# A three-block transformer kernel: at four stage changes the next stage takes up token rows 0 to 127 first

## Time and profile before

| | |
|---|---|
| median of 3 runs | 1083.47 us (1080.76 to 1084.18) |
| the profiled execution | 1084.3 us, its span 1082.3 us |
| TensorE busy | 1023.9 us, 95% of the span |
| VectorE, ScalarE, GpSimd busy | 611.3, 473.3, 352.5 us |
| HBM read | 174.6 MB |
| granted clock, mean over the span | 0.975 |

### The profile page before, as it was taken

The page is one execution under the profiler, slowest core; times in us unless marked ns, Lnnn a source line. Parts: engine busy times, 40 slices in busy tenths (PEclk is TensorE's granted clock), DMA queues, the critical chain, the costliest instruction groups (busy, mean ns, idle before and its releaser), DMA issues.

```text
span 1082.3 us, 16830 instructions
## 1 busy us (share of the span) xinstructions
PE 1023.9 (95%) x6908; PEld 897.5 (83%) x6908; DVE 611.3 (56%) x599; ACT 473.3 (44%) x606; POOL 352.5 (33%) x332
## 2 busy tenths in 40 slices
PE   7898789999999998999999999999978999999997
PEld 5886578999987877777779999987946979999986
DVE  3689855555564446354556755445467564554444
ACT  4465435444443355545454444434423554344432
POOL 3663054888899604030039910000031010000000
PEclk9999889999999999999999999999987999999999
DMA  9542014676666755443445656555971446556550
GB/s 353 170 156 78 1 43 140 217 220 216 225 210 215 244 177 160 148 159 117 138 154 159 191 158 190 194 194 192 378 267 41 143 130 191 161 191 194 178 172 39
DMA packets 130034, 186.85 MB, mean 173 GB/s; under 512 B 4672, under 2 KB 103488, under 8 KB 129344
## 3 DMA queue, kind: packets, MB, share of 16 engines
q1 hardware_dynamic: 105696, 158.34, 44.9%
q10 hardware_dynamic: 24288, 27.81, 7.7%
HBM read 174.60 MB, written 15.73 MB: 176 GB/s over the span
## 4 chain that ended last, share of the span: by engine, by line
PE 74%; DVE 11%; POOL 6%; ACT 4%; issue 3%; DMA 1%; POOLq 0%; SPq 0%; ACTq 0%; DVEq 0%
PE ps L362 11%; PE ps L364 11%; PE ps L363 11%; PE ps L405 7%; PE ps L409 7%; PE ps L407 7%; PE ps L379 3%; PE ps L381 3%; DVE cacc L1645 3%; PE ps L380 3%; DVE wlo L348 3%; PE ps L435 2%; POOL otmp L636 2%; ACT whi L342 2%; POOL ob L650 2%
## 5 line engine op out<-in xcount | busy, mean ns | idle before, releaser
L348 DVE TENSOR_TENSOR wlo<-wraw,whi 128x2048 fp32r<-128x2048 f32 x145 | 351.3, 2423 | 323.3 <-ACT whi L342 323.2
L342 ACT ACTIVATE whi<-wraw 128x2048 fp32r<-128x2048 f32 x145 | 277.5, 1914 | 294.2 <-PE ps L409 143.0
L362 PE MATMUL ps<-actH,whi 128*128 128x256 f32 x1248 | 357.8, 287 | 8.4 <-DVE wlo L348 6.3
L364 PE MATMUL ps<-actH,wlo 128*128 128x256 f32 x1248 | 354.9, 284 | 0.0
L363 PE MATMUL ps<-actL,whi 128*128 128x256 f32 x1248 | 354.8, 284 | 0.0
L362 PEld LDWEIGHTS ps<-actH,whi 128*128 128x128 f32 x1248 | 241.4, 193 | 12.4 <-DVE wlo L348 7.3
L363 PEld LDWEIGHTS ps<-actL,whi 128*128 128x128 f32 x1248 | 241.5, 194 | 0.0
L364 PEld LDWEIGHTS ps<-actH,wlo 128*128 128x128 f32 x1248 | 241.3, 193 | 0.0
L494 POOL TENSOR_SCALAR rs<-ss 128x1 f32<-128x1 f32 (+2 forms) x27 | 9.0, 334 | 611.7 <-ACT nat L477 487.0
L405 PE MATMUL ps<-whi,gH 128*128 128x512 f32 x264 | 82.3, 393 | 0.0
L409 PE MATMUL ps<-whi,gL 128*128 128x512 f32 x264 | 82.1, 392 | 0.0
(11 more groups left out here) (309 smaller groups left out, 1369.7 us busy)
## 6 DMA issues: line engine op xcount, KB each, us to landing
wraw<-in_ffn_w_gate SPq DMA_DIRECT2D x22, 1024.0 KB, 5.3
wraw<-in_ffn_w_up SPq DMA_DIRECT2D x22, 1024.0 KB, 5.3
wraw<-in_ffn_w_down SPq DMA_DIRECT2D x22, 1024.0 KB, 4.9
wraw<-in_fox_w_in SPq DMA_DIRECT2D x16, 1024.0 KB, 5.5
wraw<-in_w_gate SPq DMA_DIRECT2D x11, 1024.0 KB, 5.3
wraw<-in_w_up SPq DMA_DIRECT2D x11, 1024.0 KB, 5.6
wraw<-in_w_down SPq DMA_DIRECT2D x11, 1024.0 KB, 4.9
wraw<-in_w_in SPq DMA_DIRECT2D x10, 1024.0 KB, 7.3
```

The costliest lines, as they stand in the source:

```text
L342: act.activation(self.whi[:, n0 % RING, :], self.wraw[:, n0 % RAW, :], ACT.Copy).then_inc(self.hi_done, 1)
L348: dve.tensor_tensor(self.wlo[:, n0 % RING, :], self.wraw[:, n0 % RAW, :], self.whi[:, n0 % RING, :].bitcast(F32), ALU.subtract).then_inc(s ...
L362: pe.matmul(out, wh, self.actH[:, k, :], start=(i == 0), stop=False)
L364: last = pe.matmul(out, wl, self.actH[:, k, :], start=False, stop=(i == KT - 1))
```

## The change

- Buffers: four of `whi`, and `wlo` lies in the same four buffers as `wraw` (the low part is written over the raw unit). A load now waits until the unit four before is used up; a high part waits only for its landing.
- `mm_k_last`: the last two units of o1, f1, o2, f2, o3 and f3 are multiplied for row block 0 together, then for row block 1.
- At o1 to f1, o2 to f2 and o3 to f3 the first pair of the FFN is computed in token form (`pe_pair_rows`): row block 0 is turned in tiles of 128 tokens and multiplied with the gate and the up unit, then row block 1. The product is made from rows (`act_pair_rows`, `dve_pair_rows`) and turned by four transposes (`pe_turn_pair`) behind the next gate unit. At f1 to fox the two units fox and fox+1 are taken row block by row block in the same way.
- The diagonal is made by GpSimd (`pool_rows`). The order of norm, turn and splits in the streams of ScalarE and VectorE is new (`act_rows`, `rows`, `rows_post`).
- `keep_warm`: none before f1 and fox, 4 before f2 and f3, 17 before s as before.
- Table blocks: TensorE takes block b up after pair b+1 (blocks 0 to 9), and blocks 10 to 15 after down units 0, 2, 4, 6, 7, 8. `pool_prep` is not changed.
- fox: `wf` comes after fox+1, and the turn L1213 two quarters into fox+2. ScalarE waits for the last table stores and issues four DMAs before the first square of this change instead of after both.

```diff
-RAW = 4
-RING = 2
+RING = 4
+PREP_DOWN = (0, 2, 4, 6, 7, 8)
+FP_TURN = (0, 1, 4, 5)
...
-        self.wlo = fixed("wlo", [P, RING, UNIT], F32R)
+        self.wlo = at("wlo", [P, RING, UNIT], F32R, self.where["wraw"])
...
     def load_unit(self, sp, n0, view, it=0):
-            sp.wait_ge(self.lo_done, n - RAW + 1)
+            sp.wait_ge(self.used, n - RING + 1)
     def split_high(self, act, n0, it=0):
-        if n0 >= RING:
-            act.wait_ge(self.used, n - RING + 1)
...
+    def mm_k_last(self, pe, n0, base, xh, xl, k0, kn, waits, first, step=1):
+        for r in range(RT):
+            for u in range(2):
+                self.mm_k_pair(pe, n0 + u, base, xh, xl, k0 + 2 * u, kn, waits[u], step, (r,),
+                               first if u else first + "_half")
...
+    def act_rows(self, act, st, banks, gain, unit, post=None, base=None, first=None):
+        if post:
+            self.act_squares(act, post, self.acc_row(base, 0), 0, *self.past(first, 1))
+        else:
+            squares(0)
+        self.split_high(act, unit + 1)
+        if post:
+            squares(0)
+            self.act_squares(act, post, self.acc_row(base, 1), 1, self.used, unit)
+        self.act_turn_rows(act, st, 0, banks[0], gain)
+        self.split_high(act, unit + 2)
+        squares(1)
+        self.act_turn_rows(act, st, 1, banks[1], gain)
...
+    def pe_pair_rows(self, pe, st, n0):
+        for r in range(RT):
+            banks = self.UP_TURN[r]
+            self.pe_turn_rows(pe, st, r, banks)
+            for u in range(2):
...
+                for k in range(KT):
...
+                    pe.matmul(out, xh, wh, start=(k == 0), stop=False)
+                    pe.matmul(out, xh, wl, start=False, stop=False)
+                    last = pe.matmul(out, xl, wh, start=False, stop=(k == KT - 1))
+                    if u == 0 and k + len(banks) < KT:
+                        self.pe_turn_row(pe, st, r, k + len(banks), banks)
...
     def over_pairs(self, eng, one, prep=None):
-        one(0, 0, 0, 0)
-        if prep:
-            prep(0, 0, 0)
-        with eng.Fori(0, (FP - 1) // 2) as it:
+        for f in range(1, 3):
+            one(2 * f, f, 0, 0)
+            if prep:
+                prep(f - 1, 0, 0)
+        with eng.Fori(0, (FP - 3) // 2) as it:
             for j in range(2):
-                one(2 + 2 * j, 1 + j, it, 2)
+                one(6 + 2 * j, 3 + j, it, 2)
                 if prep:
-                    prep(1 + j, it, 2)
+                    prep(2 + j, it, 2)
...
-            if prep and i % 2 == 1:
-                self.pe_prep(pe, a, FP + i // 2)
+            if prep and i in PREP_DOWN:
+                self.pe_prep(pe, a, FP - 1 + PREP_DOWN.index(i))
...
+            def rows(st, banks, gain, base, first, unit):
+                m.residual(dve, st, base, first, unit, 0)
+                m.split_low(dve, unit + 1)
+                m.dve_turn_rows(dve, st, 0, banks[0], gain, range(4))
+                m.residual(dve, st, base, first, unit, 1)
+                m.dve_turn_rows(dve, st, 0, banks[0], gain, range(4, KT))
+                m.split_low(dve, unit + 2)
+                m.dve_turn_rows(dve, st, 1, banks[1], gain)
+            def rows_post(post, st, gain, base, unit, *gains):
+                m.dve_postnorm(dve, post, base, *gains, rows=(0,))
+                m.split_low(dve, unit + 1)
+                m.dve_turn_rows(dve, st, 0, m.UP_TURN[0], gain)
+                m.dve_postnorm(dve, post, base, *gains, rows=(1,))
+                m.split_low(dve, unit + 2)
+                m.dve_turn_rows(dve, st, 1, m.UP_TURN[1], gain)
...
                 for h in range(2):
-                    m.mm_half_k(pe, n + 2 * i + h, banks, h)
+                    for k in range(4):
+                        m.mm_quarter(pe, n + 2 * i + h, banks, h, k)
+                        if (i, h, k) == (1, 0, 1):
+                            f_turn()
```

More of the change, by code:

```diff
@@ L108, in past @@
     def past(self, name, value):
+        stage, _, kind = name.partition("_")
+        if kind in ("squares", "var", "rstd") and stage in TWO_NORMS:
+            lead, offset = TWO_NORMS[stage]
+            return self.sem(name), self.resolve(lead + "_" + kind)[1] + 2 * value + offset
         return self.sem(name), self.resolve(name)[1] + value
@@ L387, in mm_half_k, with mm_k_pair @@
             self.mm_quarter(pe, n0, banks, half, k, ready)
-    def mm_k_pair(self, pe, n0, base, xh, xl, k0, kn, waits=(), step=1, first=None):
-        pe.wait_ge(self.lo_done, n0 + 1)
+    def mm_k_pair(self, pe, n0, base, xh, xl, k0, kn, waits=(), step=1, rows=range(RT), row_done=None):
+        if 0 in rows:
+            pe.wait_ge(self.lo_done, n0 + 1)
         s = n0 % RING
-        order = [(k, r) for k in range(2) for r in range(RT)] if first is None else \
-            [(k, r) for r in range(RT) for k in range(2)]
-        for k, r in order:
+        for k, r in [(k, r) for k in range(2) for r in rows]:
             if r == 0:
@@ L409, in mm_k_pair @@
                 last = pe.matmul(self.ps[:, base + 2 * r + c, :], l, w[0][c], start=False, stop=sp_)
[L410 to L412 removed]
+        last.then_inc(self.used if RT - 1 in rows else self.sem(row_done), 1)
+    def mm_k_last(self, pe, n0, base, xh, xl, k0, kn, waits, first, step=1):
[3 more added lines that the diff above has]
+                               first if u else first + "_half")
     def tp_spot(self, kt, banks):
@@ L478, in act_squares, with act_norms @@
            .then_inc(self.sem(st + "_squares"), 1)
-    def act_norms(self, act, post, pre, base, first, used):
+    def act_norms(self, act, post, pre, base, first, used, unit=None):
         for r in range(RT):
@@ L484, in act_norms @@
             self.act_squares(act, post, self.acc_row(base, r), r, *ready)
+            if r == 0 and unit is not None:
+                self.split_high(act, unit)
         if pre:
@@ new lines, in pe_turn_pair, with act_pair_rows @@
+    def pe_turn_pair(self, pe, st):
+        pe.wait_ge(*self.past(st + "_tprod", 2))
+        for f in range(2):
+            for r in range(RT):
+                last = pe.transpose(self.ps[:, 0, f * TOK + r * P:f * TOK + (r + 1) * P],
+                                    self.prod[:, r * 256 + f * P:r * 256 + (f + 1) * P], self.ident[:])
+        last.then_inc(self.sem(st + "_tturn"), 1)
+    def act_pair_rows(self, act, st, n0):
+        for r in range(RT):
+            act.wait_ge(*(self.past(st + "_tout", 1) if r == 0 else (self.used, n0 + 2)))
+            act.activation(self.sg[:, r * 256:(r + 1) * 256], self.ps[:, self.UP_OUT[r], 0:256], ACT.Silu)\
+               .then_inc(self.sem(st + "_tsilu"), 1)
+            if r == 0:
+                self.split_high(act, n0 + 3)
@@ L525, in ffn_banks, with dve_pair_rows, pe_pair @@
+    def dve_pair_rows(self, dve, st, n0):
+        for r in range(RT):
+            c = slice(r * 256, (r + 1) * 256)
+            dve.wait_ge(*self.past(st + "_tsilu", r + 1))
+            dve.tensor_tensor(self.prod[:, c], self.sg[:, c], self.ps[:, self.UP_OUT[r], 256:512], ALU.mult)\
+               .then_inc(self.sem(st + "_tprod"), 1)
+            if r == 0:
+                self.split_low(dve, n0 + 3)
     def ffn_banks(self, a):
         return a, a + 1, (4 if a == 0 else 0)
-    def pe_pair(self, pe, st, n0, a, f0, it=0, f_step=0, ready=None):
+    def pe_pair(self, pe, st, n0, a, f0, it=0, f_step=0):
```

266 lines of the change are left out of this document (153 added, 113 removed).

## The result

The kernel after takes 1106.59 us (median of 4 runs, 1105.28 to 1113.44), the kernel before, timed beside it, 1083.5: the ratio is 1.0227, with a 95% interval of 1.0201 to 1.0252. It is slower, as forecast, but by 23 us and not by 9. The profiled execution took 1105.48 us with a span of 1103.8, against 1084.3 and 1082.3 before: 21.5 us to be placed.

What follows compares the result with a forecast made beforehand. TensorE's own work plus the places where it is held up was taken to bound the kernel. Terms from -4.2 (opening) to +8.9 (f1's tables) summed to +9.1: 1093.4 us beside the profile, 1092.6 beside the median; range 1082 to 1099.

Steps and rivals of the forecast that it cites:

- Opening: Start through o1: four buffers let splits and q head sum come earlier, 4.2 us of it carried to o1: -4.2 us.
- f1: f1's down part: six GpSimd table blocks left there make TensorE wait, +8.9 us, plus +1.2 for clock dips.
- the first dip: f1: low clock after the stall at block 10, at most 1.6 us, taken as hidden by a later stall.
- the last stall: f1's down part: TensorE waits 5 us for GpSimd's block 15.
- f1 to fox: Change from f1 to fox: late gate chain +2.3, low clock after it +1.4, late square +1.3 us.
- The gate stall: Before fox+3: the gate transpose comes later, so TensorE stalls 4.9 us; net +2.3 us.
- Its dip: fox: low clock after TensorE's 4.9 us wait before fox+3, +1.4 us (0 to 1.7).
- The store term: f1 to fox: ScalarE waits for table stores and issues four DMAs before row 0's square, +1.3 us (0 to 2.6).
- o2 to f2: Change from o2 to f2: row-by-row form takes 20.0 us against 20.7, -0.7 us (bounds -3 and +2).
- o3 to f3: Change from o3 to f3: same sum as at o2 to f2, -0.7 us (bounds -3 and +2).
- (a): Rival, stage changes: early take-up hides the whole norm chain, 12 us less than counted, 1081 to 1076; 12%.
- (c): Rival, stage changes: fewer dummy matmuls let TensorE's clock drop, five dips of 1.5 us, 1100; 14%.

Runs made afterwards that it cites:

- four mends: Kernel after with conv low parts before unit 13's, two table blocks of GpSimd lead, fox+3's split before the gate chain, row 1 before unit+2's split: 1083.6 us, ratio 1.0025.
- the lead of two blocks: Kernel before, with GpSimd's table block b waiting only for block b-2's take-up: 1079.9 us, ratio 0.9983.

## Why the forecast had the sign and not the size

Between the two profiles it is +21.5 us, and my sum was +9.1. The missing 12.4 are 5.3 in the opening, 2.8 from f1 to fox, 1.4 from o2 to f2, 2.6 in f2 and some 0.3 in the rest.

- **Opening, forecast -4.2, measured +1.1.** The largest step that failed is carrying the gain through o1. The chain moved 2.9 us at the q head sum (3.1 forecast) and 3.3 at the conv features. But I left out that the change makes unit 13's low part before the conv low parts, and that both splits stand beside GpSimd's BB tables (7.03 us for two). The wait for the conv low parts grew from 1.88 to 5.34 us, with low clock behind it. Undone, it gives 4.0. The profile before also had a long stretch at the low clock in o1 (0.50 to 146), so its own time there was no firm base: o1's first unit is 1.4 us shorter in the kernel after by that alone.
- **f1, forecast +10.1 net, measured +10.7 (and the -0.9 ahead of it).** The mechanism was right: waits of 5.3 and 3.8 us (3 and 5 forecast). That the sum fits is partly luck, as two errors cancel. From the last pair's end to f1's end it is 80.9 us, where I had 76.3 and 1.2 for the clock: block 15 is taken up 67.3 us after block 9 (some 64 forecast), and low clock follows both waits, by the granted clocks of the rows below some 4 us in all. I took the first dip as hidden by the last stall, and it isn't, since that stall counts from TensorE's own take-up of block 13. On the other side the pairs ahead became 3.7 us shorter and not 1.1, as the five waits of 0.4 us went with the later take-up. And part of the cause was missing: the second buffer is bound by its store.

```profile
322.00:326.00 4.00, 2.85 (x15) 1.95 (x16) 0.00 (x0) 0.87 (x2) 3.75 (x4) 0.50 0.03 13
326.00:330.00 4.00, 4.00 (x15) 3.13 (x14) 1.43 (x1) 3.38 (x2) 3.92 (x4) 0.70 0.51 164
...
378.00:382.00 4.00, 3.54 (x19) 2.60 (x20) 0.00 (x0) 1.44 (x3) 0.40 (x1) 0.70 0.62 227
382.00:386.00 4.00, 4.00 (x17) 3.27 (x16) 2.29 (x1) 1.24 (x1) 0.00 (x0) 0.87 0.41 83
```

- **f1 to fox, forecast +5.0, measured +7.8.** The gate stall is 4.46 us (4.9 forecast). Its dip was put at 1.4; the clock is 0.50 and 0.65 over 424 to 432, which makes some 2.5 us. Mis-sized above all is the wait for row 1's diagonal: 2.99 us, not 0.4, so that fox's row part takes 20.6 us and not 16.1. ScalarE made the high part of fox+2 ahead of row 1's square, and VectorE's low part held GpSimd's rstd. With row 1 first it is 16.5 us. The store term (+1.3) was 0 here, since the stall at block 15 and the low clock behind it give the store time; where they go it is 2.4.
- **o2 to f2, forecast -0.7, measured +0.7; o3 to f3, -0.7 and -0.7.** The wait for row 1's diagonal, 2.0 us at both, was forecast (1.6). The two changes differ by the clock, 0.79 over 586 to 594 and 1.00 behind the same wait at f3, a dip for which I had no term there. Dummies take it away.
- **f2, forecast 0, measured +2.6.** It had no step in my sum. At 639.77 a VectorE split takes 5.57 us beside a GpSimd instruction of 5.37, and TensorE waits 2.33 us. In the profiles of the changed kernels this stretch takes 179.8, 177.7 or 176.3 us, although none of their edits lies in it, and TensorE's waits for low parts in it are 2.3 to 2.4, 1.5 or 0.4 us to match. That it depends on when VectorE's splits meet GpSimd's phase tables fits these rows; no run moved that alone.
- The rivals: (a), early take-up hides the norm chain, holds a little once mended (fox 1.5 us), and not as built. (c), the clock, was right in kind for row 1's waits (1.2 and 1.3 us) and held behind f1's two table waits and the gate too.

## What to carry to other kernels

A stage that is taken up row by row puts norm chains and splits on the same engines at the same time: list, for every engine, which instruction stands ahead of the second row's first link, and put the extra units behind it. A helper that was just ahead (GpSimd's blocks, a gate chain) must be counted anew when its taker moves by one place; look for both of its releases, the take-up and the store. And before pricing a change by one profile, look for low-clock stretches behind waits in it: filling two of them in the kernel before gave 6.2 us by the medians, where the change with its four mends gave nothing.

## What the hardware showed beyond that

The kernel before has two groups of times, 1078.9 to 1080.6 us (9 of 25 runs in one series) and 1082.0 to 1086.5 (16). Profiles of both kernels differ in how long TensorE stays at the lower level of its clock (1.2 GHz, granted 0.50) behind the waits ahead of o1: until 146 in the kernel before, until about 141 in the same kernel with the lead of two blocks. The mean granted clock of the single runs goes with the groups: 0.978 or 0.979 in seven of those nine, 0.977 or less in 15 of the 16. A difference of 0.004 in the clock over 1083 us is some 4 us, which is what lies between the groups. That the stretch ahead of o1 is where they differ is likely, and not shown, since single runs have no stretches. Equal waits don't have equal effects: after 1.98 us ahead of f2's row 1 the granted clock was 0.60 over 588 to 592, after 2.00 us ahead of f3's it stayed at 1.00. The Trainium skill, TensorE: Matmul & The Clock Gate, Part 1, "What's actually happening", has the throttled state as the default, released by activity; that dummies alone bring these stretches from 0.50 to 1.00 in the kernel before agrees.
